# Output projection and layer norm as one stage, and state space outputs kept between the rotations of the next quarter

## The reference

```
x <- LayerNorm(alpha * x + mixer(x) @ w_out)
x <- LayerNorm(alpha * x + square(relu(x @ w1)) @ w2)
```

```
h[t] = a * h[t-1] + B u[t]        (complex, 32 groups of 64 states, 16 channels each)
y[t] = Re(C h[t]) + d * u[t], then gelu and a learned gate
```

## Time and profile before

| | us |
|---|---|
| median of 3 runs (4781.3 to 4788.32) | 4787.66 |
| profiled execution | 4789.65 |
| its span | 4787.9 |
| PE busy | 3965.4 (83%) |
| DVE busy | 2114.4 (44%) |
| ACT busy | 1141.5 (24%) |
| POOL busy | 687.8 (14%) |

### The profile page before, as it was taken

One profiled execution on the slowest core, in us unless ns is written; L12 is line 12 of the kernel. 1 busy time (PEld: TensorE's weight loads), 2 busy tenths in 40 slices (PEclk: granted clock), 3 DMA queues, 4 the chain that ended last, 5 costly groups with the idle time before them and its releaser, 6 DMA issues. The chain is left out here.

```text
span 4787.9 us, 65290 instructions
## 1 busy us (share of the span) xinstructions
PE 3965.4 (83%) x25189; PEld 3066.9 (64%) x25189; DVE 2114.4 (44%) x3377; ACT 1141.5 (24%) x2252; POOL 687.8 (14%) x617
## 2 busy tenths in 40 slices
PE   7978788888669599999967474844999769999995
PEld 7955566666544589989844354641447438989984
DVE  2188866666761544343443232214006253344345
ACT  1155555555500211211102020200002112111110
POOL 0044311111000211101120303030000121111102
PEclk9977799999889799999978685855995779999998
DMA  2110299999211111111110304060000201111111
GB/s 82 64 40 1 106 408 406 404 405 403 98 46 38 44 36 53 35 44 44 35 38 5 120 17 167 16 212 19 34 18 1 64 27 44 44 35 52 35 47 52
DMA packets 207051, 459.55 MB, mean 96 GB/s; under 512 B 28805, under 2 KB 113645, under 8 KB 203710
## 3 DMA queue, kind: packets, MB, share of 16 engines
q1 hardware_dynamic: 206814, 456.36, 26.1%
HBM read 440.87 MB, written 15.44 MB: 95 GB/s over the span
## 5 line engine op out<-in xcount | busy, mean ns | idle before, releaser
L1604 DVE TENSOR_TENSOR x<-x,f_d 128x512 f32<-128x512 f32 (+1 forms) x576 | 393.1, 686 | 348.2 <-PE f_d L1510 344.9
L1510 PE MATMUL f_u<-xH,f_w1h 128*128 128x364 f32 (+1 forms) x1536 | 507.5, 330 | 22.9 <-DVE f_w1l L1596 22.9
L1510 PE MATMUL f_u<-xL,f_w1h 128*128 128x364 f32 (+1 forms) x1536 | 507.3, 330 | 0.0
L1510 PE MATMUL f_u<-xH,f_w1l 128*128 128x364 f32 (+1 forms) x1536 | 507.0, 330 | 0.0
L1510 PE MATMUL f_d<-f_w2h,f_hh 128*128 128x512 f32 x1152 | 457.0, 397 | 8.8 <-DVE f_w2l L1596 8.8
L1510 PE MATMUL f_d<-f_w2h,f_hl 128*128 128x512 f32 x1152 | 456.8, 397 | 0.0
L1510 PE MATMUL f_d<-f_w2l,f_hh 128*128 128x512 f32 x1152 | 456.7, 396 | 0.0
L1583 POOL TENSOR_TENSOR f_hl<-f_h,f_hh 128x364 fp32r<-128x364 f32 (+1 forms) x192 | 184.4, 967 | 1327.9 <-ACT f_hh L1572 1327.9
L1620 DVE TENSOR_TENSOR f_h<-f_h 128x364 f32<-128x364 f32 (+1 forms) x192 | 103.2, 537 | 555.6 <-ACT f_h L1566 555.6
L1510 PEld LDWEIGHTS f_u<-xH,f_w1h 128*128 128x128 f32 x1536 | 291.0, 189 | 25.0 <-issue 23.8
L1510 PEld LDWEIGHTS f_u<-xL,f_w1h 128*128 128x128 f32 x1536 | 291.0, 189 | 1.3
(11 more groups left out here) (459 smaller groups left out, 6738.9 us busy)
## 6 DMA issues: line engine op xcount, KB each, us to landing
ss_kv<-in_cache_sb_kv SPq DMA_DIRECT2D x336, 512.0 KB, 8.2
x<-in_cache_sb_kv SPq DMA_DIRECT2D x176, 512.0 KB, 8.4
w<-in_ffn_w SPq DMA_DIRECT2D x64, 1024.0 KB, 5.5
ds_qb<-ds_q SPq DMA_DIRECT2D x24, 1024.0 KB, 6.3
ds_kc<-in_cache_dil_kv SPq DMA_DIRECT2D x16, 1024.0 KB, 7.7
x<-in_x_prompt SPq DMA_DIRECT2D x16, 512.0 KB, 7.7
pe_raw<-in_w_in_even SPq DMA_DIRECT2D x8, 1024.0 KB, 5.9
ds_kc<-in_cache_dil_kv SPq DMA_DIRECT2D x16, 512.0 KB, 6.3
```

What stands on the lines that cost most here:

```text
L1510: mm = pe.matmul(out, a, b, start=(n == 0), stop=(n == len(parts) - 1))
L1604: v.tensor_tensor(K.x[0:r, t, cs], K.x[0:r, t, cs], dn_b[(c * DOWN + u) % 4][0:r, :], ALU.add).then_inc(added, 1)
```

## The change

The output projection and the norm behind it become one stage, `project_and_norm`, in both layers. PE projects tile t and then turns tile t - 2; DVE adds, normalises and adds the bias of tile t and then takes the low part of tile t - 2; POOL and ACT follow. The projection has four banks instead of eight, the turns have four. The high part `xH` is laid over `K.xT`, whose tile has been multiplied by then (ACT waits for that), and the first feed-forward weights `w1` move to the other side of the memory. Gain, bias and `w1` are loaded at this stage's start, gain and bias ahead of the reload of x. Stage `norm_and_turn` ahead of the feed-forward is gone.

In the state space stage `keep(q - 1)` stands between `forward(q)` and `back(q)`. As it writes slices of `K.xT` earlier, the scan buffer moves to slice 7 and to the padding buffer `cpad` (whose readers raise `kd`, for which `forward(1)` waits).

```diff
-        G = y_flat[:, 2 * NT:2 * NT + 4 * QUARTER * NCH].rearrange("p (s r n) -> p s r n", s=2, r=2)
+        G = [g.rearrange("p (r n) -> p r n", r=2) for g in (y_flat[:, 3 * NT:3 * NT + 2 * QUARTER * NCH],
+                                                            cpad[:, :, :, :].rearrange("p r j c -> p (r j c)"))]
...
                     v.wait_ge(S["xc"], 4 * q + 4)
+                    if q == 1:
+                        v.wait_ge(S["kd"], 2)
...
                 for q in range(4):
                     forward(q)
+                    if q >= 1:
+                        keep(q - 1)
                     back(q)
-                    if q >= 2:
-                        keep(q - 2)
                 v.sem_inc(S["lastr"], 1)
                 sample_finals()
-                keep(2)
                 keep(3)
...
-def project_out(K, tag, weights, kt, reload):
+def project_and_norm(K, tag, weights, kt, reload, gain, bias, high_part, low, ahead):
+    LAG = 2
...
+            @block.sync
+            def _(sp):
+                sp.dma_start(gb[:, 0, :], gain.partition_broadcast(P)).then_inc(gb_loaded, 16)
+                sp.dma_start(gb[:, 1, :], bias.partition_broadcast(P)).then_inc(gb_loaded, 16)
                 if reload:
...
+                ahead.start(sp)
...
+            @block.tensor
+                def project(t):
+                    r = rows_of(t)
+                    for c in range(2):
+                        u = 2 * t + c
+                        if u >= 4:
+                            pe.wait_ge(added, u - 3)
+                        for k in range(kt):
+                            mm = pe.matmul(out_b[u % 4][0:r, :], K.xT[:, k, t * P:t * P + r], w[:, k, c * 512:(c + 1) * 512],
+                                           start=(k == 0), stop=(k == kt - 1))
+                        mm.then_inc(done, 1)
+
+                def turn(t):
+                    r = rows_of(t)
+                    pe.wait_ge(normed, t + 1)
+                    for h in range(2):
+                        u = 2 * t + h
+                        if u >= 4:
+                            pe.wait_ge(split, u - 3)
+                        for c in range(4):
+                            f = (4 * h + c) * P
+                            mm = pe.transpose(turn_b[u % 4][:, c, 0:r], K.x[0:r, t, f:f + P], K.ident[0:r, 0:r])
+                        mm.then_inc(turned, 1)
...
+                for t in range(TT + LAG):
+                    if t < TT:
+                        project(t)
+                    if t >= LAG:
+                        turn(t - LAG)
...
+            @block.vector
+                for t in range(TT + LAG):
+                    if t < TT:
+                        add(t)
+                        normalise(t)
+                        add_bias(t)
+                    if t >= LAG:
+                        split_low(t - LAG)
...
+            @block.scalar
+                for t in range(TT + LAG):
+                    if t < TT:
+                        r = rows_of(t)
+                        a.wait_ge(agg_ready, t + 1)
+                        a.activation(std[0:r, t:t + 1], agg[0:r, t, 1:2], ACT.Sqrt, bias=K.eps[0:r, :]).then_inc(std_ready, 1)
+                    if t >= LAG:
+                        s = t - LAG
+                        r = rows_of(s)
+                        for h in range(2):
+                            u = 2 * s + h
+                            a.wait_ge(turned, u + 1)
+                            if h == 0:
+                                a.wait_ge(done, 2 * s + 2)
+                            a.activation(high_part[:, 4 * h:4 * h + 4, s * P:s * P + r], turn_b[u % 4][:, :, 0:r], ACT.Copy).then_inc(high, 1)
```

More of the change, by code:

```diff
@@ L1185, in back @@
                     er, ei = E[:, 0, js, :], E[:, 1, js, :]
-                    gr_, gi_ = (quarter(G[:, q % 2, r, :]) for r in range(2))
+                    gr_, gi_ = (quarter(G[q % 2][:, r, :]) for r in range(2))
                     beside(v.tensor_tensor(quarter(pa), gr_, er, ALU.mult))
@@ L1389, in _ @@
                     mm.then_inc(done, 1)
-def project_out(K, tag, weights, kt, reload):
+def project_and_norm(K, tag, weights, kt, reload, gain, bias, high_part, low, ahead):
     nc, io = K.nc, K.io
+    LAG = 2
     with ExitStack() as ctx:
+        sb = lambda name, shape: ctx.enter_context(nc.sbuf_tensor(f"{tag}_{name}", shape, F32))
         w = weights.w
-        banks = [ctx.enter_context(nc.psum_tensor(f"{tag}_b{i}", [P, 512], F32)) for i in range(8)]
+        gb = sb("gb", [P, 2, D])
+        stats, agg, std, rstd = sb("stats", [P, TT, 2, 6]), sb("agg", [P, TT, 2]), sb("std", [P, TT]), sb("rstd", [P, TT])
+        out_b = [ctx.enter_context(nc.psum_tensor(f"{tag}_b{i}", [P, 512], F32)) for i in range(4)]
+        turn_b = [ctx.enter_context(nc.psum_tensor(f"{tag}_t{i}", [P, 4, P], F32)) for i in range(4)]
         x_loaded = [K.sem(f"{tag}_x{t}") for t in range(TT)] if reload else None
-        done, added = K.sem(tag + "_dn"), K.sem(tag + "_ad")
+        gb_loaded, done, added, steps, agg_ready, std_ready = (K.sem(f"{tag}_{n}") for n in ("gb", "dn", "ad", "dve", "agg", "std"))
+        centred, scaled, normed, turned, high, split = (K.sem(f"{tag}_{n}") for n in ("cen", "scl", "nrm", "trn", "high", "low"))
         with nc.Block() as block:
@@ L1420, in _, with add @@
+                pe.wait_ge(weights.ready, 16)
+                for t in range(TT + LAG):
[3 more added lines that the diff above has]
+                        turn(t - LAG)
             @block.vector
             def _(v):
-                for u in range(2 * TT):
-                    t, r, c = u // 2, rows_of(u // 2), (u % 2) * 512
-                    if reload and u % 2 == 0:
+                step = Chain(v, steps)
+                def add(t):
+                    r = rows_of(t)
+                    if reload:
@@ L1425, in _ @@
                         v.wait_ge(x_loaded[t], 16)
-                    v.wait_ge(done, u + 1)
-                    v.scalar_tensor_tensor(K.x[0:r, t, c:c + 512], K.x[0:r, t, c:c + 512], ALPHA, banks[u % 8][0:r, :],
-                                           ALU.mult, ALU.add).then_inc(added, 1)
+                    for c in range(2):
+                        cols = slice(c * 512, (c + 1) * 512)
+                        v.wait_ge(done, 2 * t + c + 1)
+                        v.scalar_tensor_tensor(K.x[0:r, t, cols], K.x[0:r, t, cols], ALPHA, out_b[(2 * t + c) % 4][0:r, :],
+                                               ALU.mult, ALU.add).then_inc(added, 1)
+                        v.wait_ge(added, 2 * t + c + 1)
+                        v.bn_stats(stats[0:r, t, c, :], K.x[0:r, t, cols]).then_inc(steps, 1)
+                        step.n += 1
@@ new lines, in _ @@
+                for t in range(TT + LAG):
[5 more added lines that the diff above has]
+                        split_low(t - LAG)
+            @block.gpsimd
+            def _(g):
+                g.wait_ge(gb_loaded, 32)
+                for t in range(TT):
+                    r = rows_of(t)
+                    g.wait_ge(centred, t + 1)
+                    g.tensor_tensor(K.x[0:r, t, :], K.x[0:r, t, :], gb[0:r, 0, :], ALU.mult).then_inc(scaled, 1)
@@ L2683, in program @@
             gate_and_project(K, T, weights)
-            project_out(K, "po0", weights, 8, True)
+            high, low = K.high_xT("xH0"), layer.enter_context(nc.sbuf_tensor("xL0", [P, KD, NT], F32R))
+            w1 = first_w1(K, 0)
+            project_and_norm(K, "po0", weights, 8, True, io["ln_mix_g"][0], io["ln_mix_b"][0], high[:, :, :], low[:, :, :], w1)
             weights.close()
+        feed_forward(K, "f0", 0, high[:, :, :], low[:, :, :], w1)
+        w1.close()
         layer.close()
[L2687 to L2692, removed]
         layer = ctx.enter_context(ExitStack())
@@ L2728, in program @@
         keep_dilated(K, G, weights)
-        project_out(K, "po1", weights, 6, False)
+        high, low = K.high_xT("xH1"), layer.enter_context(nc.sbuf_tensor("xL1", [P, KD, NT], F32R))
+        w1 = first_w1(K, 1)
+        project_and_norm(K, "po1", weights, 6, False, io["ln_mix_g"][1], io["ln_mix_b"][1], high[:, :, :], low[:, :, :], w1)
         weights.close()
         odd.close()
+        feed_forward(K, "f1", 1, high[:, :, :], low[:, :, :], w1)
+        w1.close()
         layer.close()
[L2733 to L2738, removed]
         outs = [io["y_prompt"][0, t * P:(t + 1) * P, :] for t in range(TT - 1)] + [io["y_sample"].rearrange("b s d -> (b s) d")]
```

44 lines of the change are left out of this document (31 added, 13 removed).

## The result

The changed kernel took 4700.97 us (median of 4 runs, 4691.79 to 4705.12) against 4787.19 before: 86.2 us less, a ratio of 0.982 with a 95% interval of 0.9808 to 0.9832. The forecast was 4700.7. The profiled execution took 4700.81 us, its span 4699.0, 88.9 less than the span before.

What follows compares the result with a forecast made beforehand. PE, busy 83% of the span, was taken as the bound, so gains lay where it idles or runs slowly. State space 10.9 + layer 0 39.3 + layer 1 37.8 - DMA 1.0 = 87.0 us: median 4700.7 us, range 4692 to 4715.

Steps and rivals of the forecast that it cites:

- PE stays the bound in the fused stage: Projection with norm: the norm chain needs 9.1 us a tile, so PE stays the bound by over 2 us a tile.
- The tails: Last addition to feed-forward: 14.6 us instead of 60.11 and 58.57, so -45.5 and -44.0 us in layers 0 and 1.
- The turns: Transposes of tiles 0 to 5 added on PE's path before the last projection: 1.03 us each, 6.2 us a layer.
- The state space stage: Second half, moved keep: the replay gains 12.3 us, less 1.4 for the clock after a 5.4 us gap: -10.9 us.
- The DMAs: Layer 1: gain, bias and w1 loads issued behind the projection's weights delay them by 1.0 us (0 to 2.6).
- Dearer turns: Rival, turns in both projections: each costs 1.4 us more, 12 of them 17 us, giving 4718 us; chance 0.07.
- No gain in the state space stage: Rival: the reorder gives nothing since DVE is the bound there, giving 4711.6 us; chance 0.07.
- PE waiting in every turn: Rival: PE waits for unnormed tiles, both projections run at 1.2 GHz, slower at 4916 us; chance 0.03.
- A serial order: Rival, fused stage: something keeps the order serial, each tile costs PE a few us, 4720 to 4760 us; chance 0.03.

Runs made afterwards that it cites:

- e4: The changed kernel with six more batch statistics (results unused) on DVE behind each of tiles 0 to 7 in both fused stages: 4707.73 us.
- e3: The changed kernel with LAG 0 instead of 2, each tile turned directly behind its own projection: 4848.97 us, ratio 1.0136 to the kernel before.
- e1: The kernel before with the state space edit alone: 4776.07 us against 4785.98, ratio 0.9981.
- e7: The changed kernel with SP waiting for the projection weights before it issues gain, bias and w1 in the fused stage: 4693.06 us in a single run.
- The second measurement: The unedited changed kernel timed again later: 4699.22 us (5 runs) against 4784.97 before (9 runs), ratio 0.9817.

## Why the prediction was right

- **PE stays the bound in the fused stage.** Right. PE is busy throughout both projections, and DVE needed 7.95 + 1.4 = 9.35 us a tile where 9.1 was forecast. e4 shows the room from the other side, e3 what happens without the lag.
- **The tails.** 14.6 us forecast, 14.39 and 14.40 measured. The steps: root at 1.67 instead of 1.52, scaling 2.19 (2.04), POOL 3.07 (2.93) for 2.33 us (2.32), bias 5.44 (5.30), low parts 6.58 (6.44), end 9.71 (9.9). From the root on each step is some 0.15 us later than counted. I put the turn of tile 8's second half at 7.9 and added 1.99 us, which in the norm before ran from the start of the whole turn. Here the whole turn starts at 7.40 and the end comes 2.31 us later: two misses that mostly cancel.
- **The turns.** 6.2 us a layer forecast, 5.3 and 4.6 measured; this term has the largest error. A turn costs 0.87 us from start to start (1474.93 to 1475.80 in layer 0), not 1.03: the change of operands that I added a little for costs nothing. The remaining 0.6 us in layer 1 are the projection's start at the lower clock, which cost less than in the execution before: in 25.29 us PE did 54 matmuls, where the earlier trace rows has 52 in 25.10.
- **The state space stage.** The replay put the third `taps` behind a gap of 1.2 us (0.83) and a gap of 5.4 us before the last `outputs` (4.97). The lower clock there cost 2.1 us, not the 1.4 that I took from `states`. Piece by piece 11.0 against 10.9; by the timed runs of e1, 9.9. The agreement of the piece is partly luck: shorter gaps and a dearer clock cancelled (13.1 - 2.1 against 12.3 - 1.4), and the replay took PE's and DVE's distance from one execution, where it moves by up to 3.9 us with the clock at the stage's start.
- **The DMAs.** Forecast 1.0, measured 0.1. I read the bias load's 7.7 us with w1 behind it against 5.1 us alone as a delay from behind. e7 excludes a delay of 1 us for the weights, and the same bias load took 5.5 to 6.2 us in other executions with w1 behind it. The ring order that the Trainium skill states (DMA: Bandwidth & Descriptors, Queues, rings and completion order) was the better guide: the 0.1 us of e7 agrees with it, and by it the sum would have been 88.0.
- **The rivals.** Dearer turns: excluded (0.87 us). No gain in the state space stage: excluded by e1. PE waiting in every turn: not in this kernel, but real at LAG 0, with the sign that was forecast and less than half the loss (63 us slower than before, not 128). A serial order: excluded by the timeline.

The errors were +0.9 and +1.6 (turns), +0.9 (DMA), +0.2 twice (tails), all forecast too slow, against a start of the state space stage that was 3.4 us longer in the profiled execution. So the agreement within 0.3 us of the first median is luck on top of a right mechanism: the edited pieces gave 3.1 us more than forecast, and the spread of code that was not edited took it back. The second measurement gives 85.8 us of gain against 87.0.

## What to carry to other kernels

Two stages that keep different engines busy are worth fusing tile by tile, and the gain can be read beforehand: the second stage's length, less its last tile's chain, less what its work costs on the first stage's busiest engine. The lag between the steps decides the sign: at lag 0 the same instructions made the kernel 1.4% slower than no fusion at all. After a fusion the tail is a chain on one engine; look there for holes (POOL's time) and for preparation of the next stage that can be done earlier, which gave another 4.5 us a layer. And an order without a wait passes on what the old one swallowed: the 3.9 us by which the start of the state space stage varies now reach its end in full.

## What the runs showed of the hardware

- PE's clock stood at the lower level after gaps of 4.97 us and of 6.8 us. It was up through gaps of 0.8 to 1.5 us. After gaps of 2.6 to 4.0 us at the start of the state space stage it was up in four executions (gaps of 3.4 to 3.6) and down for part of the next 32 transposes in eight. 36 transposes in the gap of the state space stage kept it up; the same fill ahead of the feed-forward, followed by 0.97 us of waiting, 0.71 us of turns and 2.08 us of waiting, did not. Which of these differences decides, no run here separates.
- Eight fp32 transposes of 128x128 cost 0.87 us from start to start between matmuls of another shape at the full clock, and 1.76 us (1449.37 to 1451.13 in e3) at the lower one.
- POOL's multiplication of 128x1024 took 2.33 to 2.35 us alone and 2.35 beside DVE operations with one operand in PSUM, but 3.27 beside a DVE addition of two SBUF operands.
- The same code ahead of the first `taps` took 69.5 to 73.4 us in twelve profiled executions, the shortest four being those in which its second 32 transposes ran at the full clock (3.71 us).
